# Dense heads of a hybrid encoder: the next head's projections one step fewer, its meta scores one step sooner

## The chip, the cores and the metric

The kernel runs on one core of a Trainium2 chip. The metric is device time in microseconds (us) for one execution of the whole program, median of the runs shown. TensorE is called PE in the profile (its weight loads PEld), VectorE DVE, ScalarE ACT, GpSimd POOL, and the queue of SyncE that issues DMAs SP.

## What is computed

The reference is an encoder trunk of two layers over 1024 real tokens and 16 meta tokens. Each layer is one mixer with three groups of heads side by side: A (window attention), B (dense attention over all tokens) and C (a gated recurrence). The change touches group B alone. Cut to that group:

```python
DEPTH = 2; SEQ = 1024; N_META = 16; BLOCK = 128; HEAD_DIM = 64
B_HEADS = 4; B_QK_DIM = HEAD_DIM; B_V_DIM = 2 * HEAD_DIM

def diff_attention(q, k, v, lam, key_ok):
    """q/k (B,Lp,H,2,d), v (B,Lp,H,2d); dense bidirectional, swept over 128-query blocks."""
    ...
    def attend(q_blk):
        s = jnp.einsum('bqhcd,bkhcd->bhcqk', q_blk, k).astype(jnp.float32) * scale
        s = jnp.where(key_ok, s, NEG)
        p = jax.nn.softmax(s, axis=-1)
        a = p[:, :, 0] - lam * p[:, :, 1]
        return jnp.einsum('bhqk,bkhv->bqhv', a.astype(v.dtype), v)

# in mixer_layer, h = x @ w_in:
qb = rotary(qb.reshape(bsz, lp, 2 * B_HEADS, B_QK_DIM), cos, sin)
kb = rotary(kb.reshape(bsz, lp, 2 * B_HEADS, B_QK_DIM), cos, sin)
ob = diff_attention(qb, kb, vb, lam, valid)
ob = rms_norm(ob, subln_w.reshape(B_HEADS, B_V_DIM)) * (1.0 - lam_init)
yb = ob.reshape(bsz, lp, B_WIDTH).astype(dt) * jax.nn.silu(gb)
```

Each head has two score components. Their softmaxes are combined with a factor lam, and the result weighs the values.

## The kernel before

The kernel has one hand-written instruction stream for each engine, joined by semaphores. The order in a stream is the order of the code; no scheduler moves anything. Matrix products are made in three matmuls each (hi times hi, hi times lo, lo times hi).

Group B is done head by head, in four passes B0 to B3 (`pass_b`). A pass has one step for each block of 128 query tokens: nine in layer 0 (steps 0 to 8, the last one holds the 16 meta tokens as queries) and eight in layer 1 (steps 0 to 7). In the code n is this number and t the step. In step t of head g the engines do the following.

- PE: the scores of the step after (`scores`, twelve matmuls, L1103), then, once DVE has combined the probabilities of step t, nine transposes of them (`transposes`, L1259, in groups 0, 1 and 2) and nine products with the values (`values`, L1275). Between the groups of transposes it makes parts of the projection of the next head nx (`project`, L931).
- ACT: copies of the transposed probabilities (`evac_probs`, L1611), the exponentials of the step after (`exps`, L1599 and L1601, first component 0, then 1), the copy of the output (`values_out`, L1621) and its norm.
- DVE: the maximum of each score component (`maximum`, L2123 and L2124), work for the next head, the output of the step before (`finish`, L2149 and L2152), and the combination of the two components of the step after (`combine`, L2133 to L2139; the long one is L2137).

The next head's queries and keys are projected in units (f, j): piece j of three pieces of tokens (0, 1, 2), f = 0 and 1 for the two halves of each rotated pair. A unit is made in two half-projections of twelve matmuls each. `b_steps` hands them out: it makes the list of halves, divides it over n - 3 steps, and notes for each step which units DVE rotates (`turned`, one step after the unit is complete: `qk_rope`, L2062 to L2068) and which pieces are then split into hi and lo (`rounded`: `qk_hi_of` on ACT, L1574, and `qk_lo` on DVE, L2076). Between rotation and split lie four DMAs of SP for each piece (`place_qk`, from `rot` to `qk_t`). Units (0, 0) and (1, 0) of a head are made at the end of the pass before last, in steps n - 2 and n - 1 (`early`, `after_next`); pass B2 has none to make there, and pass B3 has no next head. The number of half-projections in steps 0, 1, 2, ... is 2, 2, 1, 1, 1, 1, 0, 2, 2 in layer 0 and 2, 2, 2, 1, 1, 0, 2, 2 in layer 1, with 0 in the last two steps of B2.

The scores of the 16 meta keys are made for a whole head at once. In step n - 2, once its keys are complete, DVE copies the meta keys (`meta_keys`, L2087), PE multiplies them with all queries (`meta_scores`, L1213, into banks 6 and 0), and ACT copies the rows to `meta_rows` (L1580). In step n - 1, PE turns the rows (`meta_turned`, L1224, in layer 0 also L1228), ACT copies them to `meta_s` (`meta_out`, L1588 and L1589), and DVE makes their bound (`meta_bound`, L2097 to L2102), which `maximum` needs for the next head's first scores. These stand ahead of the step's other work on each of the three engines. The PSUM banks are given out in the same order by `bank_plan`.

The place of the turning in PE's stream is

```python
scores(b_step(l, g, t, 1))
if nx and t == q_tiles(l) - 1:
    meta_turned(l, nx)
pe.wait_ge(b_comb, B_STEP[l, g, t])
transposes(t, 0)
```

## Time and profile before

| | us |
|---|---|
| median of 3 runs | 1710.3 |
| lowest and highest run | 1707.62, 1711.12 |
| the profiled execution | 1706.29 |
| its span | 1705.0 |
| PE busy in it | 1567.1 |
| DVE, ACT, POOL busy | 1080.7, 875.4, 410.1 |

All times in the rows are from the start of the profiled span. The dense passes of layer 0 lie between about 500 and 798 us, those of layer 1 between about 1338 and 1604. A row of a timeline gives the start, the length from the first to the last of the instructions merged in it, the engine, the line, the operation, what it writes and reads, and their number. A bracket at its end is the time that the engine was idle before it, and what ended that. A row of a window gives the busy time of each engine in it. A timeline can count twice as many values (L1275) as the program's order, since the profile holds two records for each.

### The profile page before, as it was taken

To read this page: it belongs to the slowest core of one execution; us is meant where nothing else is said; L and a number is where in the kernel's file an instruction comes from. 1 tells how busy PE (TensorE), PEld (TensorE's weight loads), DVE (VectorE), ACT (ScalarE), POOL (GpSimd) and SP (SyncE) were. 2 spreads that over 40 slices of the span, in tenths; PEclk is the share of its full clock that TensorE was granted. 3 is DMA by queue.
4 is the path that set the end of the run, shared out by engine and by line. 5 is a ranking of instruction groups with operands and counts; after the bars stand their busy time and mean duration, and the time that the engine had idled before them with its cause. 6 is when DMAs were issued, how large, how long until landed. Compare 5 with 4: busy or idle time off the path is not lost.

```text
span 1705.0 us, 38582 instructions
## 1 busy us (share of the span) xinstructions
PE 1567.1 (92%) x15296; PEld 1463.2 (86%) x15296; DVE 1080.7 (63%) x2461; ACT 875.4 (51%) x2569; POOL 410.1 (24%) x390
## 2 busy tenths in 40 slices
PE   2899999999999989889989999999999899987996
PEld 2899999999888878668989999999999789876896
DVE  6477585446557777775255766844455678787527
ACT  4444545355617676775035445452464477677404
POOL 5333141220121002020453423213103101112044
PEclk9899999999999999999999999999999999999998
DMA  7111201200120111042122102012002111114312
GB/s 264 39 53 37 63 27 32 83 26 14 36 86 17 49 25 49 18 157 99 60 75 83 56 14 64 27 36 78 29 11 71 52 25 50 50 27 146 117 51 100
DMA packets 97859, 102.32 MB, mean 60 GB/s; under 512 B 7504, under 2 KB 87744, under 8 KB 97424
## 3 DMA queue, kind: packets, MB, share of 16 engines
q1 hardware_dynamic: 96720, 98.78, 18.0%
q8 instruction: 123, 2.02, 0.5%
q10 hardware_dynamic: 960, 1.07, 0.2%
q14 instruction: 56, 0.46, 0.1%
HBM read 70.14 MB, written 21.17 MB: 54 GB/s over the span
## 4 chain that ended last, share of the span: by engine, by line
PE 58%; DVE 19%; ACT 11%; POOL 5%; issue 4%; DMA 3%; SPq 0%; ACTq 0%; DVEq 0%; POOLq 0%
PE psum L931 42%; ACT p_b L1601 3%; PE psum L1275 3%; DVE p_b L2137 3%; PE psum L1103 3%; PE psum L1259 3%; POOL w_lo L896 2%; DVE row_max L2123 2%; DVE s_a L1990 2%; PE psum L1000 2%; ACT aT_b L1611 1%; ACT pT_a L1517 1%; POOL w_hi L892 1%; PE psum L978 1%; DMA w_raw<-in_w_in 1%
## 5 line engine op out<-in xcount | busy, mean ns | idle before, releaser
L931 PE MATMUL psum<-w_hi,hT_hi 128*128 128x256 f32 x1824 | 523.6, 287 | 9.4 <-POOL w_lo L896 8.1
L931 PE MATMUL psum<-w_hi,hT_lo 128*128 128x256 f32 x1824 | 513.7, 282 | 0.0
L931 PE MATMUL psum<-w_lo,hT_hi 128*128 128x256 f32 x1824 | 513.5, 282 | 0.0
L892 POOL CAST w_hi<-w_raw 128x512 fp32r<-128x512 f32 (+1 forms) x168 | 112.3, 668 | 1147.8 <-DMA w_raw<-in_w_in 679.6
L931 PEld LDWEIGHTS psum<-w_hi,hT_hi 128*128 128x128 f32 x1824 | 344.2, 189 | 18.5 <-POOL w_lo L896 10.0
L931 PEld LDWEIGHTS psum<-w_hi,hT_lo 128*128 128x128 f32 x1824 | 344.3, 189 | 0.0
L931 PEld LDWEIGHTS psum<-w_lo,hT_hi 128*128 128x128 f32 x1824 | 344.2, 189 | 0.0
L931 PE MATMUL psum<-hT_hi,w_hi 128*128 128x346 f32 (+1 forms) x672 | 226.4, 337 | 9.5 <-DVE hT_lo L1728 9.4
L896 POOL TENSOR_TENSOR w_lo<-w_raw,w_hi 128x512 fp32r<-128x512 f32 (+1 forms) x168 | 215.7, 1284 | 24.1 <-DVE neg_max L2124 12.0
L931 PE MATMUL psum<-hT_hi,w_lo 128*128 128x346 f32 (+1 forms) x672 | 218.1, 325 | 0.0
L931 PE MATMUL psum<-hT_lo,w_hi 128*128 128x346 f32 (+1 forms) x672 | 217.8, 324 | 0.0
L2123 DVE TENSOR_REDUCE row_max<-psum 128x1 f32<-128x1024 f32 x136 | 165.6, 1218 | 16.7 <-PE psum L1103 16.4
L1275 PE MATMUL psum<-vg_b,aT_b 128*128 128x128 f32 (+1 forms) x1224 | 157.1, 279 | 10.0 <-ACT aT_b L1611 10.0
L1275 PEld LDWEIGHTS psum<-vg_b,aT_b 128*128 128x128 f32 (+1 forms) x1224 | 142.8, 186 | 17.4 <-ACT aT_b L1611 14.0
L1601 ACT ACTIVATE p_b<-psum,neg_max 128x1024 f32<-128x1024 f32 x136 | 150.1, 1103 | 0.0
L931 PEld LDWEIGHTS psum<-hT_hi,w_hi 128*128 128x128 f32 x672 | 128.5, 191 | 11.9 <-issue 10.9
L1611 ACT COPY aT_b<-psum 128x384 f32<-128x384 f32 (+1 forms) x204 | 87.6, 463 | 90.9 <-PE psum L1259 89.7
L931 PEld LDWEIGHTS psum<-hT_hi,w_lo 128*128 128x128 f32 x672 | 128.8, 192 | 0.0
L931 PEld LDWEIGHTS psum<-hT_lo,w_hi 128*128 128x128 f32 x672 | 128.3, 191 | 0.0
L1103 PE MATMUL psum<-qk_b 64*128 64x512 f32 (+1 forms) x816 | 113.1, 408 | 13.7 <-ACT p_b L1601 13.3
L1259 PEld LDWEIGHTS psum<-ident,p_b 128*128 128x128 f32 (+1 forms) x612 | 66.3, 140 | 58.1 <-DVE p_b L2137 35.4
L1259 PE MATMUL psum<-ident,p_b 128*128 128x128 f32 (+1 forms) x612 | 92.4, 277 | 25.1 <-DVE p_b L2137 16.9
(179 smaller groups left out, 2382.5 us busy)
## 6 DMA issues: line engine op xcount, KB each, us to landing
w_raw<-in_w_in SPq DMA_DIRECT2D x72, 256.0 KB, 3.8
w_raw<-in_w_in SPq DMA_DIRECT2D x28, 512.0 KB, 4.4
h_dram<-hbuf SPq DMA_DIRECT2D x16, 512.0 KB, 2.6
w_raw<-in_w_out SPq DMA_DIRECT2D x16, 512.0 KB, 4.3
hbuf<-h_dram SPq DMA_DIRECT2D x16, 512.0 KB, 6.2
qk_b<-y_dram SPq DMA_DIRECT2D x16, 512.0 KB, 3.3
y_dram<-y_stage SPq DMA_DIRECT2D x96, 64.0 KB, 1.6
qk_t<-rot SPq DMA_DIRECT2D x56, 86.5 KB, 2.2
```

Source lines behind the costliest of these rows:

```text
L892: pool.tensor_copy(hi, raw).then_inc(w_hi_done, 1)
L896: pool.tensor_tensor(lo, raw, hi.bitcast(F32), ALU.subtract).then_inc(w_split, 1)
L931: last = nc.tensor.matmul(out_ap, lhs[a](k), rhs[b](k), start=k == 0 and a + b == 0, stop=k == KT - 1 and b == 1)
L1000: return nc.tensor.matmul(o_ap, k_sel[rs, k_at:k_at + H_ROWS], q_ap, start=True, stop=True)
L1103: last = [nc.tensor.matmul(out_of(r), q_of(a, r), k_of(b, r), start=i == 0, stop=i == 2) for r in range(2)]
L1259: last = nc.tensor.transpose(psum[:, b, i * P:i * P + m], p0_b[0:m, B_STEP[l, g, t] % 2, k * P:(k + 1) * P], ident[0:m, 0:m])
L1275: last = nc.tensor.matmul(psum[0:m, b, 0:P], aT_b[:, k, 0:m], vg_b[:, head_no(g), k, 0:P], start=k == 0, stop=k == TILES - 1)
L1601: nc.scalar.activation(probs[:, 0:REAL * P].rearrange("p (i n) -> p i n", i=2), psum[0:m, b:b + 2, :], ACT.Exp, scale=SCALE, bias=neg_max[ ...
L1611: nc.scalar.copy(aT_b[:, 3 * j:3 * j + 3, 0:m], psum[:, b, 0:3 * P].rearrange("p (k c) -> p k c", k=3)[:, :, 0:m])\
L1990: then(nc.vector.tensor_tensor_reduce(s_a[0:m, i, h, 0:w], psum[0:m, bank(key), 0:w], band_sb[0:m, band_columns(t)], 1.0, NEG, ALU.add, AL ...
L2123: then(nc.vector.tensor_reduce(row_max[0:m, i, c:c + 1], psum[0:m, b:b + 2, :], AX.XY, ALU.max))
L2137: stt(p0_b[0:m, i, 0:TOK], p1_b[0:m, :], coef[0:m, j, 0:1], p0_b[0:m, i, 0:TOK], ALU.mult, ALU.add).then_inc(b_comb, 1)
```

## The change

The halves are divided over n - 4 steps instead of n - 3, and the last piece is split one step sooner (`b_steps`). Half-projections per step become 2, 2, 2, 1, 1, 0, 0, 2, 2 in layer 0 and 2, 2, 2, 2, 0, 0, 2, 2 in layer 1. The meta keys, their scores and the copy of the rows move from step n - 2 to n - 3. Turning, copy and bound move from n - 1 to n - 2: on PE behind the first two groups of transposes, on ACT behind the third copy of probabilities, on DVE behind the maxima. The scores go into banks 6 and 7. For heads B1 to B3 ACT writes the rows into `rot`, the buffer of the rotation. In step n - 2 the second half-projection no longer stands behind the values.

```diff
@@ b_steps
-        q, r = divmod(len(halves), n - 3)
+        q, r = divmod(len(halves), n - 4)
...
-            rounded[min(t + 2, n - 2)] += [j for _, (f, j) in turned[t] if f]
+            rounded[min(t + 2, n - 3)] += [j for _, (f, j) in turned[t] if f]
@@ bank_plan
-                if nx and t == n - 1:
-                    add(("meta", l, nx), 6)
                 add(("aT", l, g, t, 0), 0)
                 add(("aT", l, g, t, 1), 1)
+                if nx and t == n - 2:
+                    add(("meta", l, nx), 6)
...
-                if nx and t == n - 2:
-                    for i, b in enumerate((6, 0)):
-                        add(("metaT", l, nx, i), b)
+                if nx and t == n - 3:
+                    for i in range(2):
+                        add(("metaT", l, nx, i), 6 + i)
@@ meta_rows_of
+        if g != "B0":
+            return rot[0:2 * META].rearrange("p a n -> p (a n)")[:, 0:REAL * P]
@@ tensor, pass_b
-                if nx and t == q_tiles(l) - 1:
-                    meta_turned(l, nx)
                 pe.wait_ge(b_comb, B_STEP[l, g, t])
                 transposes(t, 0)
                 transposes(t, 1)
+                if nx and t == q_tiles(l) - 2:
+                    meta_turned(l, nx)
                 for h, x, half in parts[:1]:
                     project(l, h, "qk", x, half)
                 transposes(t, 2)
-                late = nx and t == q_tiles(l) - 2
                 for h, x, half in parts[1:2]:
-                    if not late:
-                        project(l, h, "qk", x, half)
+                    project(l, h, "qk", x, half)
...
-                if late:
-                    for h, x, half in parts[1:2]:
-                        project(l, h, "qk", x, half)
+                if nx and t == q_tiles(l) - 3:
                     meta_scores(l, nx)
@@ scalar, pass_b
-                if nx and t == q_tiles(l) - 1:
-                    meta_out(l, nx)
...
+                if nx and t == q_tiles(l) - 2:
+                    meta_out(l, nx)
                 if after:
                     exps(after, 1)
...
-                if nx and t == q_tiles(l) - 2:
+                if nx and t == q_tiles(l) - 3:
                     meta_rows_out(l, nx)
@@ vector, pass_b
-                if after and after[1] == 0:
-                    meta_bound(l, after[0])
...
+                if nx and t == q_tiles(l) - 3:
+                    meta_keys(l, nx)
                 if nx and t == q_tiles(l) - 2:
-                    meta_keys(l, nx)
+                    meta_bound(l, nx)
```

PE in the end of pass B2 of layer 0, before. The first row is the end of step 6; `psum<-qk_b` are scores, `ident,p_b` transposes, `vg_b,aT_b` values, and a row x9 of transposes holds all three groups.

```order
L1275 MATMUL psum<-vg_b,aT_b 128x128 x9
L1103 MATMUL psum<-qk_b 16x512 x12
L1259 MATMUL psum<-ident,p_b 128x128 x9
L1275 MATMUL psum<-vg_b,aT_b 128x128 x9
L1213 MATMUL psum<-qk_b,meta_k 32x512 x6
L1103 MATMUL psum<-qk_b 128x512 x12
L1224 MATMUL psum<-ident,meta_rows 128x32 x8
L1228 MATMUL psum<-meta_k,qk_b 16x32 x3
L1259 MATMUL psum<-ident,p_b 128x16 x9
L1275 MATMUL psum<-vg_b,aT_b 16x128 x9
```

The same place in the changed kernel, from the values of step 6 on.

```order
L1277 MATMUL psum<-vg_b,aT_b 128x128 x9
L1215 MATMUL psum<-qk_b,meta_k 32x512 x6
L1105 MATMUL psum<-qk_b 16x512 x12
L1261 MATMUL psum<-ident,p_b 128x128 x6
L1226 MATMUL psum<-ident,rot 128x32 x8
L1230 MATMUL psum<-meta_k,qk_b 16x32 x3
L1261 MATMUL psum<-ident,p_b 128x128 x3
L1277 MATMUL psum<-vg_b,aT_b 128x128 x9
L1105 MATMUL psum<-qk_b 128x512 x12
L1261 MATMUL psum<-ident,p_b 128x16 x9
```

The meta scores stand ahead of the scores of step 8 now instead of ahead of the next head's, and the turning stands behind two groups of step 7's transposes instead of ahead of step 8's.

DVE in step 4 of pass B1 of layer 1, before: the maxima of step 5, the lo half of piece 1, the finish of step 3 and the start of the combination.

```order
L2123 TENSOR_REDUCE row_max<-psum 128x1
L2124 SCALAR_TENSOR_TENSOR neg_max<-row_max,meta_max 128x1
L2123 TENSOR_REDUCE row_max<-psum 128x1
L2124 SCALAR_TENSOR_TENSOR neg_max<-row_max,meta_max 128x1
L2076 TENSOR_TENSOR qk_b<-qk_t,qk_b 128x2x346
L2149 SCALAR_TENSOR_TENSOR coef<-rstd,inv_sum 128x1
L2152 SCALAR_TENSOR_TENSOR y_stage<-o_b,coef,vg_b 128x128
```

The same step in the changed kernel.

```order
L2121 TENSOR_REDUCE row_max<-psum 128x1
L2122 SCALAR_TENSOR_TENSOR neg_max<-row_max,meta_max 128x1
L2121 TENSOR_REDUCE row_max<-psum 128x1
L2122 SCALAR_TENSOR_TENSOR neg_max<-row_max,meta_max 128x1
L2074 TENSOR_TENSOR qk_b<-qk_t,qk_b 128x2x346
L2063 TENSOR_TENSOR rot<-psum,rope_sb 128x346
L2064 TENSOR_TENSOR psum<-psum,rope_sb 128x346
L2065 TENSOR_TENSOR rot<-rot 128x346
L2066 TENSOR_TENSOR rot<-rot,psum 128x346
L2147 SCALAR_TENSOR_TENSOR coef<-rstd,inv_sum 128x1
L2150 SCALAR_TENSOR_TENSOR y_stage<-o_b,coef,vg_b 128x128
```

The four operations of the second rotation of piece 2 came from step 5 to step 4, behind the lo half of piece 1.

## Rows read from the trace of the kernel before

**Rows 1.** Page, part 1: busy us (share of the span) and instructions of each engine.

```profile
PE 1567.1 (92%) x15296; PEld 1463.2 (86%) x15296; DVE 1080.7 (63%) x2461; ACT 875.4 (51%) x2569; POOL 410.1 (24%) x390
```

**Rows 2.** Timeline of PE, pass B1 of layer 1: start us, length us, then the instruction.

```profile
1429.54 0.88 PE L1259 MATMUL psum<-ident,p_b 128*128 128x128 f32 x6
...
1436.48 1.65 PE L1103 MATMUL psum<-qk_b 64*128 64x512 f32 x12
1438.06 0.87 PE L1259 MATMUL psum<-ident,p_b 128*128 128x128 f32 x6
...
1443.21 1.65 PE L1103 MATMUL psum<-qk_b 64*128 64x512 f32 x12
...
1477.21 1.65 PE L1103 MATMUL psum<-qk_b 64*128 64x512 f32 x12
```

**Rows 3.** Timeline of DVE, the same pass: start us, length us, then the instruction.

```profile
1429.65 1.23 DVE L2123 TENSOR_REDUCE row_max<-psum 128x1 f32<-128x1024 f32 x1 [1.49 <-PE psum L1103]
...
1436.40 1.30 DVE L2137 SCALAR_TENSOR_TENSOR p_b<-p_b,coef 128x1040 f32<-128x1040 f32 x1
...
1438.16 1.22 DVE L2123 TENSOR_REDUCE row_max<-psum 128x1 f32<-128x1024 f32 x1 [0.39 <-PE psum L1103]
...
1443.83 1.30 DVE L2137 SCALAR_TENSOR_TENSOR p_b<-p_b,coef 128x1040 f32<-128x1040 f32 x1
...
1451.20 1.30 DVE L2137 SCALAR_TENSOR_TENSOR p_b<-p_b,coef 128x1040 f32<-128x1040 f32 x1
```

**Rows 4.** Timeline of DVE, combinations in B1 of layer 0, then in B0 of layer 1.

```profile
605.38 1.30 DVE L2137 SCALAR_TENSOR_TENSOR p_b<-p_b,coef 128x1040 f32<-128x1040 f32 x1
...
612.50 1.30 DVE L2137 SCALAR_TENSOR_TENSOR p_b<-p_b,coef 128x1040 f32<-128x1040 f32 x1
...
627.01 1.30 DVE L2137 SCALAR_TENSOR_TENSOR p_b<-p_b,coef 128x1040 f32<-128x1040 f32 x1
...
1369.27 1.30 DVE L2137 SCALAR_TENSOR_TENSOR p_b<-p_b,coef 128x1040 f32<-128x1040 f32 x1
...
1377.51 1.30 DVE L2137 SCALAR_TENSOR_TENSOR p_b<-p_b,coef 128x1040 f32<-128x1040 f32 x1
```

**Rows 5.** Timeline of DVE, end of B2 and first steps of B3, layer 0.

```profile
701.00 1.30 DVE L2137 SCALAR_TENSOR_TENSOR p_b<-p_b,coef 128x1040 f32<-128x1040 f32 x1
...
708.12 1.30 DVE L2137 SCALAR_TENSOR_TENSOR p_b<-p_b,coef 128x1040 f32<-128x1040 f32 x1
...
716.24 1.29 DVE L2137 SCALAR_TENSOR_TENSOR p_b<-p_b,coef 16x1040 f32<-16x1040 f32 x1
...
721.19 1.23 DVE L2123 TENSOR_REDUCE row_max<-psum 128x1 f32<-128x1024 f32 x1
...
726.37 1.30 DVE L2137 SCALAR_TENSOR_TENSOR p_b<-p_b,coef 128x1040 f32<-128x1040 f32 x1
...
733.97 1.30 DVE L2137 SCALAR_TENSOR_TENSOR p_b<-p_b,coef 128x1040 f32<-128x1040 f32 x1
...
740.80 1.30 DVE L2137 SCALAR_TENSOR_TENSOR p_b<-p_b,coef 128x1040 f32<-128x1040 f32 x1
```

**Rows 6.** Timeline of PE, layer 0: the first scores in B2, then its end.

```profile
653.38 1.65 PE L1103 MATMUL psum<-qk_b 64*128 64x512 f32 x12
...
716.69 1.67 PE L1103 MATMUL psum<-qk_b 64*128 64x512 f32 x12
718.29 0.68 PE L1224 MATMUL psum<-ident,meta_rows 32*128 32x32 f32 x8
...
724.27 1.05 PE L1275 MATMUL psum<-vg_b,aT_b 128*16 128x128 f32 x6 [2.74 <-ACT aT_b L1611]
725.76 2.74 PE L1103 MATMUL psum<-qk_b 64*128 64x512 f32 x12 [0.43 <-ACT p_b L1601]
```

**Rows 7.** Windows: length, busy PE, PEld, DVE, ACT, POOL, granted clock, DMA share, GB/s.

```profile
1468.05:1477.21 9.16, 9.16 (x72) 8.49 (x71) 5.62 (x17) 5.07 (x13) 0.00 (x0) 1.00 0.03 8
724.70:728.20 3.50, 3.07 (x16) 2.10 (x14) 1.92 (x5) 2.04 (x7) 0.00 (x0) 0.51 0.69 205
```

## The prediction, made before the changed kernel was run

> **What bounds the kernel now.** I read the page first. TensorE is busy for 1567.1 of 1705.0 us [rows 1], so an edit is worth what it adds to or takes from TensorE's idle time in the stretch that it touches. All its matmuls stay. I then read the dense passes step by step, on the timelines of PE and DVE. "comb(t)" is the start of the L2137 row of step t, "S(t)" the start of the twelve L1103 matmuls that make step t's scores, which TensorE issues in step t-1.
>
> Two limits alternate. With two half-projections a step is bound by TensorE: one such step lies between the L1259 rows at 1429.54 and 1438.06, 8.52 us [rows 2], with no idle time noted in it. With one or none it is bound by the ring DVE combine, transposes, ACT copies and exponentials, combine: 7.12 to 7.43 us from comb to comb in the steps with one half-projection [rows 3, 4], 6.83 in pass B3 with none [rows 5], while TensorE has about 6.6 and 4.7 us of work (8.52 less one or two half-projections of some 1.9, below). So a half-projection is free in a step bound by the ring, and costs where it makes TensorE the bound.
>
> The last step of a pass holds the chain that the change goes for: scores, turned rows, ACT's copy of them, DVE's bound, then the maximum. DVE's first maximum for the next head starts at 721.19 [rows 5], where the scores issued at 716.69 [rows 6] would have let it start at 718.37 (1.68 after S, as from 1436.48 in [rows 2] to 1438.16 in [rows 3]): 2.8 us late. But in five of six passes the question is whether TensorE waits for it. In pass B1 of layer 1 it does not: busy 9.16 of 9.16 us in that step [rows 7]. In B2, whose last two steps have no projections, it does: 2.74 us idle before the matmuls at 724.27, and then the granted clock falls to the lower level, 1.2 of 2.4 GHz (0.51 in [rows 7]); the scores at 725.76 take 2.74 us for 1.65 [rows 6].
>
> So the rows show a gap to win in one pass of each layer, and none in the others. The Trainium skill, page Perfetto Trace Analysis, section Optimization Strategy, says to find the gaps of the bound engine and to make what they wait for start sooner. That is what the change does; by that rule the late maximum is won back wherever it stands, which is rival (a), and by [rows 7] there is nothing to win where TensorE has no gap.
>
> **Layer 0, the front of a pass.** Half-projections per step go from 2,2,1,1,1,1,0,2,2 to 2,2,2,1,1,0,0,2,2. Up to step 5 that is exactly what layer 1 does before the change, so layer 1 is the template. comb(3) to comb(4) is 612.50 - 605.38 = 7.12 us in layer 0's B1, a step on the ring, and so it is in B0. In layer 1 it is 1377.51 - 1369.27 = 8.24 in B0, +1.1, and 1443.83 - 1436.40 = 7.43 in B1, +0.3 [rows 3, 4]. In B2 DVE is the later one in both layers: 0. The step that loses its half-projection stays on the ring: 0.
>
> **Layer 0, the end of B0 and B1.** The lo half of the keys, the copies to meta_k and the meta scores now lie in step 6, without projections. For this step B2's step 7 is the template, since it has none either: comb(7) to comb(8) 716.24 - 708.12 = 8.12 us, and S, behind the meta scores, follows 0.45 later, at 716.69 [rows 5, 6]. From comb(6) at 627.01 [rows 4]: + 8.12 + 0.45, then a full step of TensorE 8.52 plus the turned rows (0.68 in [rows 6], about 0.8 with its three extra matmuls), then 8.52 again, is 653.4 for S(1) of the next head. Before it is 653.38 [rows 6]. So +0.0 to +0.3 each; I take +0.1. What the last step gains, step 6 pays: it has nothing left to hide the wait for meta_k.
>
> **Layer 0, the end of B2.** Here the chain is exposed. Before: from comb(6) at 701.00 to comb(1) of B3 at 733.97, 32.97 us [rows 5]. After: 8.12 for step 6; step 7: S at +0.45, maximum 1.68 later, then from first maximum to combine 726.37 - 721.19 = 5.18 us, and, as an estimate from the 0.68 us of turned rows and the 0.45 above, 0.5 each for ACT's copy and DVE's bound between maximum and combine: 8.3; then two plain ring steps of 740.80 - 733.97 = 6.83. Sum 30.1 us: -2.9. Of this about 0.8 is the slow clock: comb to comb is 733.97 - 726.37 = 7.60 there and 6.83 after.
>
> **Layer 1, B0 and B1.** The counts go from 2,2,2,1,1,0,2,2 to 2,2,2,2,0,0,2,2, and no template exists. Step 3 gets its second half-projection and becomes bound by TensorE: S(5) moves from 1443.21 to 1438.06 + (1436.48 - 1429.54) = 1445.00 [rows 2], which is also the price of a half-projection, 1.79 us here, and 0.1 to 0.2 more where it fills no small wait. Step 4 now holds the lo half of piece 1 and the second rope of piece 2 together on DVE, which step 2 also has: from its first maximum at 1429.65 to the combine at 1436.40 is 6.75 us [rows 3]. So comb(5) = 1445.00 + 1.68 + 6.75 = 1453.43. Before it is at 1451.20: 2.2 later. Step 5 takes the 8.12 us of the keys' step, comb(6) = 1461.55. Then S(7) at 1462.00, + 8.52 + 0.68 + 8.52 = 1479.7 for S(1) of the next head, against 1477.21 [rows 2]: +2.5. Two passes: +5.0. The edit moves a half-projection from a step with room into one without, and puts two DVE jobs into one step: TensorE then stands idle in steps 4 and 5 with nothing issued to cover it.
>
> The bounds: if step 4's work on DVE found room and TensorE's slack took the rest, each pass would cost 0. If every growth added up, it would be 1.79 in step 3, 6.75 + 1.30 (the L2137 row) - 7.37 = 0.68 in step 4 and 8.12 - 7.12 = 1.0 in step 5: 3.5. I take the 2.5 of the path traced, since each of its pieces is a row.
>
> **Layer 1, B2.** The same 2.2 at comb(5), less the end's gain of layer 0 without the clock, 2.1: +0.1.
>
> Edits at nothing: meta rows in rot (nothing else is in it then: the last piece's DMAs have landed before ACT's hi copy, and the next rope waits for a projection behind the turned rows); the changed banks 6, 7 (both were released by the rope a step earlier); SP's copies of piece 2 a step sooner (the hi copy waits for the landing, which has as long as it had; if late, it adds to the 8.12).
>
> **Sum.** 1.1 + 0.3 + 0.2 - 2.9 + 5.0 + 0.1 = +3.8 us. The profiled execution took 1706.29 us, 1.3 of it around the span, and would take 1710.1; the median of the three runs is 1710.3, 4.0 above that execution, and the difference is carried over to it: 1714.1.
>
> **Rivals.** (a) Faster: the end chain does count in all six passes, and the 2.8 us of the late maximum come back six times, 16.8 us: 1693.5. For it: the chain is there in every pass. Against: [rows 7], TensorE full. It decides once TensorE waits in that step for more than what step 5 or 6 newly loses, about 2 us. (b) Layer 1 loses nothing, since step 4's two DVE jobs find room: 1.1 + 0.3 + 0.2 - 2.9 + 0 - 2.1 = -3.4: 1706.9. For it: DVE is idle in part of every step. Against: 6.75 us in step 2 is a chain without a wait. (c) The clock. In layer 0 the scores after a 2.74 us idle gap ran at the lower level of the granted clock [rows 6, 7]. Layer 1's two steps without projections could bring such a drop into each pass: 3 x 1.1 and the 0.8 that B2 no longer saves: 1714.1 + 4.1 = 1718.2. Against: the gaps that I work out for these steps are under 2 us. The Trainium skill, page TensorE: Matmul & The Clock Gate, section HAM oscillation — how this bites in real kernels, says that waits in which TensorE idles bring its clock down and that each costs again. By that rule (c) is a real danger, and the drop of layer 0 agrees with it.
>
> **The numbers.** The forecast, +3.8 with +1.5 to +6.5, 0.65; (a) 0.07; (b) 0.14; (c) 0.14. Runs of this kernel can be told apart from about 0.2%, 3.4 us. Faster is (a) and a third of (b): 0.11. Within 0.2% is two fifths of the forecast and the rest of (b): 0.36. Slower is the rest: 0.53. The range reaches from (b) to (c): 1707 to 1718.5; (a) is left out, and so are the outer halves of (b) and (c).
>
> **What would show it.** In layer 1, B0 and B1: comb(4) to comb(5) near 9.6 us instead of 7.4, comb(5) to comb(6) near 8.1 instead of 7.1, and the last two steps shorter, with the pass 2 to 3 us longer. In layer 0's B2: the combine before the next head 7 us after its predecessor instead of 10.1, no clock record at half there. In B0 and B1 the last step shorter by two, and step 6 longer by 1. I am wrong if the layer 1 passes don't grow, or if TensorE was waiting in the last steps after all.

## The result and the profile after

| | before | after |
|---|---|---|
| median of 20 runs each, on one chip | 1709.95 | 1714.43 |
| ratio after to before, 95% interval | | 1.003, 1.0022 to 1.0039 |
| the profiled execution, its span | 1706.29, 1705.0 | 1715.02, 1713.7 |
| mean granted clock of that execution | 0.990 | 0.988 |

The change costs 4.5 us by the medians. These are over all runs; the ratios, here and below, leave out the few slow runs (one of before here, at 2025 us). First the place that the forecast put the most on, pass B1 of layer 1. These are DVE's combinations (L2135 in the changed kernel, L2137 before) of steps 3 to 7, then the maximum and combinations that open the next head:

```profile
1442.76 1.30 DVE L2135 SCALAR_TENSOR_TENSOR p_b<-p_b,coef 128x1040 f32<-128x1040 f32 x1
...
1450.18 1.30 DVE L2135 SCALAR_TENSOR_TENSOR p_b<-p_b,coef 128x1040 f32<-128x1040 f32 x1
...
1459.67 1.30 DVE L2135 SCALAR_TENSOR_TENSOR p_b<-p_b,coef 128x1040 f32<-128x1040 f32 x1
...
1467.85 1.30 DVE L2135 SCALAR_TENSOR_TENSOR p_b<-p_b,coef 128x1040 f32<-128x1040 f32 x1
...
1476.78 1.30 DVE L2135 SCALAR_TENSOR_TENSOR p_b<-p_b,coef 128x1040 f32<-128x1040 f32 x1
1479.33 1.23 DVE L2121 TENSOR_REDUCE row_max<-psum 128x1 f32<-128x1024 f32 x1 [1.18 <-PE psum L1105]
...
1485.00 1.30 DVE L2135 SCALAR_TENSOR_TENSOR p_b<-p_b,coef 128x1040 f32<-128x1040 f32 x1
```

From comb(4) to comb(5) it is now 9.49 us where it was 7.37 [rows 3], and to comb(6) 8.18. On PE the same stretch reads (timeline; L1105 are scores, L1261 transposes, L1277 values, L1215 the meta scores):

```profile
1451.36 1.65 PE L1105 MATMUL psum<-qk_b 64*128 64x512 f32 x12
...
1456.86 0.94 PE L1277 MATMUL psum<-vg_b,aT_b 128*128 128x128 f32 x6 [0.82 <-ACT aT_b L1609]
1458.34 1.65 PE L1105 MATMUL psum<-qk_b 64*128 64x512 f32 x12 [0.55 <-ACT p_b L1599]
1461.02 0.88 PE L1261 MATMUL psum<-ident,p_b 128*128 128x128 f32 x6 [1.04 <-DVE p_b L2135]
...
1466.77 1.57 PE L1215 MATMUL psum<-qk_b,meta_k 128*32 128x512 f32 x6 [1.52 <-DVE meta_k L2085]
```

S(5) is at 1451.36, 1.18 behind comb(4). Before it was at 1443.21, 0.62 ahead of it [rows 2, 3]. And TensorE, with no projections in these two steps, waits 0.82, 0.55, 1.04 and 1.52 us in the rows shown. The gain at the end is there too: the last step, from 1476.78 to 1485.00, takes 8.22 us for 10.37, and the next head's first maximum, at 1479.33, starts 1.69 behind its scores (1477.64), without the lateness of before. The step ahead of it, from 1467.85, is not shorter but longer, 8.93 for 8.59.

Next the end of B2 in layer 0, DVE from comb(6) to comb(1) of the next head, the answer to [rows 5]:

```profile
703.95 1.30 DVE L2135 SCALAR_TENSOR_TENSOR p_b<-p_b,coef 128x1040 f32<-128x1040 f32 x1
...
712.14 1.30 DVE L2135 SCALAR_TENSOR_TENSOR p_b<-p_b,coef 128x1040 f32<-128x1040 f32 x1
...
721.92 1.29 DVE L2135 SCALAR_TENSOR_TENSOR p_b<-p_b,coef 16x1040 f32<-16x1040 f32 x1
723.21 1.20 DVE L2121 TENSOR_REDUCE row_max<-psum 128x1 f32<-128x1024 f32 x1
...
728.37 1.30 DVE L2135 SCALAR_TENSOR_TENSOR p_b<-p_b,coef 128x1040 f32<-128x1040 f32 x1
...
735.19 1.30 DVE L2135 SCALAR_TENSOR_TENSOR p_b<-p_b,coef 128x1040 f32<-128x1040 f32 x1
```

The maximum of the next head follows at once on the combination (723.21), and that step takes 6.45 us instead of 10.13. But the step from 712.14 to 721.92 takes 9.78. PE's timeline shows why. The first window is the stretch ahead of the meta scores, the other two give the clock at the same place of B0 and here (columns as in [rows 7]; the sixth figure after the length is the granted clock):

```profile
711.05 2.60 PE L1215 MATMUL psum<-qk_b,meta_k 128*32 128x512 f32 x6 [1.52 <-DVE meta_k L2085]
713.58 2.05 PE L1105 MATMUL psum<-qk_b 64*16 64x512 f32 x12
```

```profile
705.25:711.05 5.80, 3.79 (x27) 3.10 (x27) 4.24 (x12) 5.13 (x15) 0.00 (x0) 1.00 0.16 40
...
561.10:564.50 3.40, 3.40 (x10) 1.10 (x12) 2.29 (x7) 1.85 (x6) 0.00 (x0) 0.50 0.07 19
711.30:714.70 3.40, 3.40 (x12) 1.08 (x12) 2.11 (x6) 1.67 (x4) 0.00 (x0) 0.50 0.07 19
```

Behind the 1.52 us wait for the meta keys the granted clock is at 0.50, the lower level of 1.2 GHz. The six meta scores take 2.60 us for the 1.57 that they take at 1466.77, and the scores behind them 2.05 (1.57 at full clock, at 638.10 in B1). The drop that [rows 7] showed at 724.7 is gone, and two others have come, this one and one at 561 in B0. Of the six waits of this kind in the changed kernel (one in each pass, all 1.52 us long) two are followed by a drop, though TensorE is busy for 3.79 or 3.80 of the 5.80 us ahead of each of the six. In B2 the kernel before has the same wait one step later, and no drop behind it, so the rows from which the forecast built this stretch ran at full clock. On PE's timeline of before:

```profile
715.19 1.57 PE L1213 MATMUL psum<-qk_b,meta_k 128*32 128x512 f32 x6 [1.52 <-DVE meta_k L2087]
```

The passes one by one. A pass is taken from comb(1) of its head to comb(1) of the next, B0 from comb(0), so that the ends of the passes count where they are felt; for B1 of layer 1 after the change that is 1493.86 - 1424.91 = 68.95:

```profile
1424.91 1.30 DVE L2135 SCALAR_TENSOR_TENSOR p_b<-p_b,coef 128x1040 f32<-128x1040 f32 x1
...
1493.86 1.30 DVE L2135 SCALAR_TENSOR_TENSOR p_b<-p_b,coef 128x1040 f32<-128x1040 f32 x1
```

The forecast's terms stand beside the difference.

| us | before | after | difference | forecast |
|---|---|---|---|---|
| layer 0, B0 | 79.14 | 81.78 | +2.6 | +1.2 |
| layer 0, B1 | 73.61 | 74.04 | +0.4 | +0.4 |
| layer 0, B2 | 72.93 | 71.47 | -1.5 | -2.9 |
| layer 1, B0 | 73.18 | 75.26 | +2.1 | +2.5 |
| layer 1, B1 | 65.82 | 68.95 | +3.1 | +2.5 |
| layer 1, B2 | 64.54 | 64.59 | +0.05 | +0.1 |
| sum | 429.2 | 436.1 | +6.9 | +3.8 |

The rest of the program, whose code the change leaves alone, differs by 1.8 us between these two executions (8.7 of span less 6.9). Such a difference says nothing of the change: the changed kernel profiled a second time (changed_again below) has the same dense passes to 0.1 us and a span of 1708.1, 5.6 us less than here.

### The profile page after: what moved, and what is told of

It is laid out like the page before. It is cut to its first block, busy times and chain, and to the rows that moved or that the text cites. A ratio compares the mean times of both kernels' runs of the same rounds, so it can differ in the third digit from the quotient of the medians.

```text
span 1713.7 us, 38582 instructions
## 1 busy us (share of the span) xinstructions
PE 1573.2 (92%) x15296; PEld 1463.7 (85%) x15296; DVE 1081.2 (63%) x2461; ACT 875.4 (51%) x2569; POOL 409.8 (24%) x390
## 3 DMA queue, kind: packets, MB, share of 16 engines
q10 hardware_dynamic: 960, 1.07, 0.2%
## 4 chain that ended last, share of the span: by engine, by line
PE 60%; DVE 18%; ACT 10%; POOL 5%; issue 3%; DMA 3%; SPq 0%; ACTq 0%; DVEq 0%; POOLq 0%
PE psum L933 43%; PE psum L1277 4%; PE psum L1105 4%; PE psum L1261 3%; ACT p_b L1599 3%; POOL w_lo L898 2%; DVE p_b L2135 2%; ACT aT_b L1609 2%; DVE s_a L1988 2%; DVE row_max L2121 2%; PE psum L1002 2%; POOL w_hi L894 1%; ACT pT_a L1515 1%; PE psum L980 1%; DMA w_raw<-in_w_in 1%
## 5 line engine op out<-in xcount | busy, mean ns | idle before, releaser
L1277 PE MATMUL psum<-vg_b,aT_b 128*128 128x128 f32 (+1 forms) x1224 | 158.8, 279 | 8.9 <-ACT aT_b L1609 8.9
L1277 PEld LDWEIGHTS psum<-vg_b,aT_b 128*128 128x128 f32 (+1 forms) x1224 | 143.6, 186 | 17.8 <-ACT aT_b L1609 14.1
L1105 PE MATMUL psum<-qk_b 64*128 64x512 f32 (+1 forms) x816 | 112.9, 408 | 13.9 <-ACT p_b L1599 13.8
L1261 PEld LDWEIGHTS psum<-ident,p_b 128*128 128x128 f32 (+1 forms) x612 | 65.8, 140 | 57.4 <-DVE p_b L2135 26.8
L1261 PE MATMUL psum<-ident,p_b 128*128 128x128 f32 (+1 forms) x612 | 92.7, 278 | 22.2 <-DVE p_b L2135 13.1
```

The source lines that it names most:

```text
L1105: last = [nc.tensor.matmul(out_of(r), q_of(a, r), k_of(b, r), start=i == 0, stop=i == 2) for r in range(2)]
L1261: last = nc.tensor.transpose(psum[:, b, i * P:i * P + m], p0_b[0:m, B_STEP[l, g, t] % 2, k * P:(k + 1) * P], ident[0:m, 0:m])
L1277: last = nc.tensor.matmul(psum[0:m, b, 0:P], aT_b[:, k, 0:m], vg_b[:, head_no(g), k, 0:P], start=k == 0, stop=k == TILES - 1)
```

## The experiments

All ratios are to the kernel before, run beside it on the same chip, with 95% intervals. "Layer 0" and "layer 1" are sums of three passes as in the table above (before: 225.7 and 203.5; after: 227.3 and 208.8). The texts written ahead of the runs name kernels by labels: e4_filler is experiment 4, e6_split_bound is 7, e7_b2_only is 8, e9_b2_filler is 9 and e11_bound_and_filler is 11.

**1. The distribution of the halves alone.** Edit to the kernel before; meta scores, turning and bound stay where they were.

```diff
-        q, r = divmod(len(halves), n - 3)
+        q, r = divmod(len(halves), n - 4)
```

> Only the half-projections are handed out one step sooner; the meta scores, their turning and their bound stay where they were before. Theory (a half-projection is free on the ring and costs in a step bound by TensorE, and layer 1's step 4 gets two DVE jobs): layer 0 +1.4 us as in its front, layer 1 comb(5) 2.2 later in each pass and step 5 then 0.3 shorter, so +1.9 in each of three passes: about +7 us against the kernel before, more than the whole change. Rival (moving halves costs nothing, what costs is the moved meta work): 0, within 0.1%.

Measured: 1716.77 (1.0039, 1.0023 to 1.0055); layer 0 +0.5, layer 1 +6.0. Combinations of steps 4 to 7 and 0 of the next head in B1 of layer 1:

```profile
1450.09 1.30 DVE L2137 SCALAR_TENSOR_TENSOR p_b<-p_b,coef 128x1040 f32<-128x1040 f32 x1
...
1459.57 1.30 DVE L2137 SCALAR_TENSOR_TENSOR p_b<-p_b,coef 128x1040 f32<-128x1040 f32 x1
...
1466.31 1.30 DVE L2137 SCALAR_TENSOR_TENSOR p_b<-p_b,coef 128x1040 f32<-128x1040 f32 x1
...
1474.89 1.30 DVE L2137 SCALAR_TENSOR_TENSOR p_b<-p_b,coef 128x1040 f32<-128x1040 f32 x1
...
1485.25 1.30 DVE L2137 SCALAR_TENSOR_TENSOR p_b<-p_b,coef 128x1040 f32<-128x1040 f32 x1
```

Step 4 costs 9.48 us here as in the full change, step 5, without the meta keys, 6.74, and the last step keeps its 10.36. Pass by pass (B0, B1, B2 of layer 1) the halves alone cost 1.6, 2.1 and 2.3 us, the full change 2.1, 3.1 and 0.05. So most of the loss comes from the halves, but not all of it: the sooner chain adds 0.5 and 1.0 in B0 and B1, where step 5 takes 8.18 us for 6.74 and the next head's first step 8.9 for 8.0, more than the last step gives back (8.22 for 10.36). In B2 the chain takes 2.3 back, and 0.9 of that is clock: in this trace alone the clock fell at 1551 us, and the first step of B3 takes 7.73 us for the 6.84 of before.

```profile
1552.34 1.30 DVE L2137 SCALAR_TENSOR_TENSOR p_b<-p_b,coef 128x1040 f32<-128x1040 f32 x1
...
1560.07 1.30 DVE L2137 SCALAR_TENSOR_TENSOR p_b<-p_b,coef 128x1040 f32<-128x1040 f32 x1
```

Layer 0 lost 0.5 us and not the 1.4 expected. The front came as expected, but step 6, left without a half-projection, takes 6.74 us for 7.12, 0.4 less in each of the three passes. The forecast has this term at 0.

**2 and 3. The change in one layer only.** Each place that the change touches asks for the layer and takes the old form in the other:

```diff
+SOONER = {0}
-        q, r = divmod(len(halves), n - 4)
+        q, r = divmod(len(halves), n - 4 if l in SOONER else n - 3)
...
```

> The whole change in layer 0 alone, layer 1 as before. By the forecast's sum: 1.1 + 0.3 + 0.2 - 2.9 = -1.3 us against before. By the trace of the changed kernel, where two scores or meta scores rows in step 6 of layer 0 ran at the lower clock: +1.6 us, if these drops come in most executions. Rival: the cost of the change is spread over both layers alike: +2.5.

> The whole change in layer 1 alone, layer 0 as before. By the forecast and by the trace of the changed kernel: +5.1 us against before (2.5 in B0, 2.5 in B1, 0.1 in B2). Rival, alike in both layers: +2.5.

Measured: layer 0 only 1709.17 (0.9993, 0.9978 to 1.0007), with layer 0 at -1.4 and layer 1 at -0.1 in its trace; layer 1 only (the same with {1}) 1716.21 (1.0041, 1.0025 to 1.0057), with +5.2 in layer 1. In the first trace the clock fell at none of the three waits of layer 0: the six meta scores take 1.57, 1.57 and 1.59 us there. The same code at the same waits had two drops in the trace of the full change. So -1.4 is what layer 0 gains where no new drop comes, almost to the tenth the forecast's sum for it (1.1 + 0.3 + 0.2 - 2.9 = -1.3). It holds pass by pass too: B0 +1.2, B1 +0.4, B2 -3.0, for +1.2, +0.4 and -2.9. Against this trace the full change is 1.5 longer in B0 and 1.5 in B2, the price of a drop.

**4. Work in place of the wait.** Six matmuls that nobody reads, ahead of TensorE's wait for the meta keys of heads B1 to B3, in the changed kernel:

```diff
         def meta_scores(l, g):
+            if g != "B0":
+                wait_free(pe, ("metaT", l, g, 0))
+                for _ in range(6):
+                    nc.tensor.matmul(psum[0:2 * META, bank(("metaT", l, g, 0)), :], hT_hi[:, 0:2 * META],
+                                     hT_hi[:, 0:512], start=True, stop=True)
             pe.wait_ge(b_keys, 4 * B_HEAD[l, g])
```

> The changed kernel, with six extra matmuls of 32x512 (their result is overwritten) in the wait of step n - 3 for the copies to meta_k, where TensorE stands idle for 1.52 us. They take some 1.3 us, so they should hide in the wait. If the granted clock falls because of the idle time in steps 5 and 6 of layer 0, the drops at 561 and 711 us go and the time falls by 1.5 us for each, 2 to 3 us below the changed kernel. If the drops have another cause, or don't come often, it stays as the changed kernel, +5 us against before.

Measured: 1710.85 (1.0009, 0.9996 to 1.0022). The end of B0 of layer 0 on PE's timeline and the clock there:

```profile
558.56 1.62 PE L1213 MATMUL psum<-hT_hi 128*32 128x512 f32 x6
560.32 1.59 PE L1220 MATMUL psum<-qk_b,meta_k 128*32 128x512 f32 x6
561.84 1.57 PE L1105 MATMUL psum<-qk_b 64*16 64x512 f32 x12
```

```profile
558.50:562.00 3.50, 3.36 (x17) 1.37 (x18) 3.12 (x11) 3.16 (x11) 0.00 (x0) 1.00 0.08 23
```

The filler takes 1.62 us (1.3 were expected) in a place where TensorE waited 1.52, the meta scores start no later (7.10 us behind comb(6) with it and without), and they run at full clock. Layer 0 comes to 224.56, 2.7 us less than in the changed kernel, and layer 1, which had no drop, stays at 208.79. The median is 3.6 below the changed kernel's (the intervals of these two ratios touch at 1.0022). So the work added costs nothing. That it holds the clock is not shown by this one trace, since experiment 2 had no drop in layer 0 either. The means over the runs speak for it: a granted clock of 0.991 here (11 runs) against 0.988 for the changed kernel (32 runs, its repeat below included).

**5 and 6. What makes step 4 of layer 1 longer.** First, DVE's second job taken out of it: piece 1 is split a step sooner.

```diff
@@ b_steps, the changed kernel
+        if l == 1:
+            rounded[3].append(rounded[4].pop(rounded[4].index(1)))
```

> The changed kernel, but in layer 1 the hi and lo split of piece 1 is done in step 3 instead of 4, so that step 4 holds only the second rotation of piece 2 on DVE, and step 3, where DVE waits for late scores anyway, takes the split. If the two DVE jobs in step 4 are part of the loss, comb(4) to comb(5) falls from 9.5 to about 8.7 us (less the 0.8 of the lo half) and layer 1 gains 0.8 in each of three passes: 2.4 us below the changed kernel. If step 4 is long only because its scores come late behind the second half-projection, it stays at 9.5.

Then, the half-projection taken out of step 3 (nine of its twelve matmuls are left out, three are left):

```diff
@@ tensor, project, the changed kernel
+            if l == 1 and half == 1 and x == (1, 2):
+                ks = [KT - 1]
```

> The changed kernel with 9 of the 12 matmuls left out of the second half of layer 1's unit (1, 2), which step 3 makes (the keys of piece 2 are so incomplete). TensorE is freed of 1.45 us in the step which the forecast calls bound by TensorE. If that is what makes comb(5) late, comb(4) to comb(5) falls from 9.5 to 8.05 us, and layer 1 by 1.45 in each pass, 4.3 us below the changed kernel. Rival: the ring and DVE set step 4, and the freed time turns into a wait of TensorE: 0.

Measured, from comb(4) to comb(5) of B1: 7.37 before, 9.49 after, 8.44 with the split sooner, 8.07 with the half-projection gone. The rows of DVE for the last two, the split first:

```profile
1448.63 1.30 DVE L2137 SCALAR_TENSOR_TENSOR p_b<-p_b,coef 128x1040 f32<-128x1040 f32 x1
...
1457.07 1.30 DVE L2137 SCALAR_TENSOR_TENSOR p_b<-p_b,coef 128x1040 f32<-128x1040 f32 x1
```

```profile
1450.18 1.30 DVE L2137 SCALAR_TENSOR_TENSOR p_b<-p_b,coef 128x1040 f32<-128x1040 f32 x1
...
1458.25 1.30 DVE L2137 SCALAR_TENSOR_TENSOR p_b<-p_b,coef 128x1040 f32<-128x1040 f32 x1
```

Both causes are there. Without the half-projection the step falls by 1.42, and 0.70 stay over the old 7.37, where the prediction's bounds put the second job of DVE at 0.68. Without the second job it falls by 1.05, 1.07 stay, and step 3 grows by 0.26. So the half-projection alone makes 1.07, the second job alone 0.70, and both together 2.12, which is 0.35 more than their sum. Whole kernels: 1712.62 (1.002, 1.0007 to 1.0034) with the split sooner, layer 1 at 206.38, 2.4 less than after; and 1710.92 (1.0007, 0.9992 to 1.0022) without the half-projection, where B1 of layer 1 is 1.4 shorter than after, while B0 and B2 of it show no gain: in that execution the clock fell behind the waits for the meta keys of just these two passes (its six meta scores take 2.60 and 2.71 us there), and at no place of layer 0, where this kernel is the same as the changed one.

**7. The bound alone, without moving anything else.** In the kernel before, the part of `meta_bound` for a component stands behind that component's first maximum, which no longer waits for it:

```diff
@@ vector, maximum, the kernel before
+                if t == 0 and g != "B0":
+                    meta_bound(l, g, [c])
@@ vector, pass_b
-                if after and after[1] == 0:
-                    meta_bound(l, after[0])
```

> The kernel before, with one edit of its own: the bound of the next head's meta scores is made for one component at a time, behind the reduction of that component's scores, not for both ahead of it. The exponentials of the next head's first step can start 1.4 to 2 us sooner. TensorE waits for them only at the end of the B2 passes: -1.4 and the 0.8 of the slow clock in layer 0, -1.3 in layer 1, and 0.3 in layer 0's B0, where comb(0) of B1 came late: 3 to 4 us below the kernel before. If the late maximum cost TensorE time in every pass, it would be 1.4 six times, 8 us or more. If it costs nothing anywhere, 0.

Measured: 1708.34 (0.9991, 0.998 to 1.0003); layer 0 -1.4, layer 1 -1.0, the latter in B2 alone. This tests rival (a) by itself. Of the 2.8 us of the late maximum it wins 1.3 to 1.7 in each last step. In B1 of layer 1 the last step does shrink: combinations of steps 7 and 0 of the next head, and the window of the stretch between them:

```profile
1470.40 1.30 DVE L2139 SCALAR_TENSOR_TENSOR p_b<-p_b,coef 128x1040 f32<-128x1040 f32 x1
...
1479.48 1.30 DVE L2139 SCALAR_TENSOR_TENSOR p_b<-p_b,coef 128x1040 f32<-128x1040 f32 x1
```

```profile
1471.70:1480.70 9.00, 9.00 (x73) 8.29 (x73) 6.71 (x18) 5.10 (x13) 0.00 (x0) 1.00 0.11 26
```

It is 9.08 us instead of 10.37, and the pass is 65.90 instead of 65.82: TensorE was busy for all of the stretch, so DVE's earlier combination waits for it in the steps behind. The 1.3 us come back only where TensorE stood idle, in B2 (last step 10.13 to 8.77 in layer 0, 9.65 to 8.19 in layer 1). The passes give 2.3 us and the medians 1.1, less than the 3 to 4 expected. A part is that in layer 0 the clock still fell behind the end of the pass (0.8 of the sum expected).

**8 to 12. The change only where it gains.** The whole change for head B3 of layer 0 (made in pass B2), and the split bound of the kernel above for all others (b2_only):

```diff
+SOONER = {(0, "B3")}
-        q, r = divmod(len(halves), n - 4)
+        q, r = divmod(len(halves), n - 4 if (l, nx) in SOONER else n - 3)
...
```

> The whole change in pass B2 of layer 0 alone, the only pass in which the forecast has it gain (-2.9), and in all other passes the kernel before with the split bound of e6_split_bound. Expected 4.5 us below the kernel before (2.9 + 1.3 + 0.3), 1706 by the median. Rival: front and end of B2 eat what e6_split_bound gives there, no better than that kernel.

Measured: 1705.35 (0.9978, 0.9966 to 0.9991). The median is 4.1 us below the kernel before, for 4.5 expected. Layer 0 comes to 223.70, layer 1 to 203.78. The clock fell behind the wait for the meta keys at 709 us, and also at 1535 in B2 of layer 1, where this kernel has the order of before. Then come four more kernels: the same with the six matmuls of the filler ahead of that wait, for head B3 of both layers (9, b2_filler); the changed kernel again (10, changed_again); the split bound and the filler without any change of order (11, bound_and_filler); and b2_only again (12, b2_again):

> The change kept for the last head of layer 0's third pass alone, the bound split by component in the other heads (both as in e7_b2_only), and six matmuls with no reader (one 32x512 product per component, of sizes as in e4_filler) put on TensorE ahead of its wait for the meta keys in that one head. Theory (the wait for the meta keys lets the granted clock fall at that step, which costs about 1.5 us where it happens, and the filler takes that wait's place): no clock record at half between 700 and 715 us, the six meta scores 1.6 us and not 2.6, the pass over the third head of layer 0 about 1.4 us shorter than in e7_b2_only (71.27 to about 69.9), and the time 0.5 to 1.5 us below e7_b2_only's 1705.35, so a ratio of about 0.997. Rival (the clock falls at times that no step decides, and the filler only adds its own 1.6 us less the wait of 1.5): the time of e7_b2_only within 0.3 us.

> The changed kernel once more, unedited, beside e9_b2_filler on the same chip. Theory (its place in the program and not chance makes the clock fall in the step that makes the meta scores): records at half near 561 and near 711 us again, dense segments of layer 1 again 5.2 us longer than before's, and a ratio of 1.003. Rival (those two drops were this one execution's): neither record there, and layer 0's dense heads 1.4 us shorter than before's, with the ratio still near 1.002.

> The kernel before with the bound split by component (as in e6_split_bound) and the six matmuls with no reader ahead of the wait for the meta keys of the fourth head, in both layers: e9_b2_filler without the changed order of layer 0's third pass. Theory (the changed order is worth 0.7 us in that pass where no clock drop disturbs either, and the late bound leaves TensorE idle a step later, where the clock still falls): a record at half near 725 us, the pass over layer 0's third head about 71.9 us against 69.74 in e9_b2_filler, layer 1 as in e9_b2_filler, and the time some 2 us above the 1700.12 of e9_b2_filler: ratio 0.996. Rival (the filler and the split bound alone did it): within 0.7 us of e9_b2_filler.

> e7_b2_only once more, unedited, on the same chip as e11_bound_and_filler: e9_b2_filler came out 5.2 us below it in another call, of which the dense segments of the two traces show 3.0 (1.5 in the third pass of each layer, where e7's clock fell). Theory (a part of the 5.2 is chance between executions): 1704 to 1706 here, and a drop at half near 709 us again, while the one near 1535 us need not come back. Rival (the filler is worth 5 us): 1705 again with both drops.

| | median | ratio, interval | layer 0 | B2 of it | layer 1 |
|---|---|---|---|---|---|
| b2_only | 1705.35 | 0.9978, 0.9966 to 0.9991 | 223.70 | 71.27 | 203.78 |
| b2_again | 1705.45 | 0.9973, 0.9964 to 0.9983 | 223.67 | 71.21 | 202.40 |
| bound_and_filler | 1705.92 | 0.9983, 0.9974 to 0.9992 | 224.51 | 72.10 | 202.65 |
| b2_filler | 1700.12 | 0.9947, 0.9935 to 0.9959 | 222.14 | 69.74 | 202.30 |
| changed_again | 1714.24 | 1.0025, 1.0013 to 1.0037 | 227.32 | 71.49 | 208.73 |

b2_filler has five runs, the others twelve each. The changed kernel's dense passes repeat to the tenth, with its two drops in the same two passes: 557.05 and 707.03 are the meta scores of B0 and B2 in its trace.

```profile
557.05 2.53 PE L1215 MATMUL psum<-qk_b,meta_k 128*32 128x512 f32 x6 [1.52 <-DVE meta_k L2085]
...
632.55 1.59 PE L1215 MATMUL psum<-qk_b,meta_k 128*32 128x512 f32 x6 [1.52 <-DVE meta_k L2085]
...
707.03 2.36 PE L1215 MATMUL psum<-qk_b,meta_k 128*32 128x512 f32 x6 [1.52 <-DVE meta_k L2085]
```

With change and filler (b2_filler) the end of B2 runs at full clock throughout, from comb(6) to comb(1) of the next head:

```profile
700.98 1.30 DVE L2160 SCALAR_TENSOR_TENSOR p_b<-p_b,coef 128x1040 f32<-128x1040 f32 x1
...
709.17 1.30 DVE L2160 SCALAR_TENSOR_TENSOR p_b<-p_b,coef 128x1040 f32<-128x1040 f32 x1
...
717.43 1.29 DVE L2160 SCALAR_TENSOR_TENSOR p_b<-p_b,coef 16x1040 f32<-16x1040 f32 x1
...
723.88 1.30 DVE L2160 SCALAR_TENSOR_TENSOR p_b<-p_b,coef 128x1040 f32<-128x1040 f32 x1
...
730.77 1.30 DVE L2160 SCALAR_TENSOR_TENSOR p_b<-p_b,coef 128x1040 f32<-128x1040 f32 x1
```

29.79 us, where the prediction's working for this stretch gave 30.1 and the changed kernel needs 31.24. The filler without the change of order (bound_and_filler) does not do it: TensorE then runs dry one step later, and the scores of the next head are slow.

```profile
721.23 0.83 PE L1280 MATMUL psum<-vg_b,aT_b 128*16 128x128 f32 x6 [0.78 <-ACT aT_b L1616]
723.33 2.50 PE L1103 MATMUL psum<-qk_b 64*128 64x512 f32 x12 [1.27 <-ACT p_b L1606]
```

So in this pass the two parts need each other: the order moves the chain away from the pass's end, and with the filler no drop came behind the wait for the meta keys. B2 is 2.4 us shorter with both than with the filler alone (69.74 against 72.10), and 1.5 shorter than with the order alone. This kernel beats the one before by 0.5% and the changed one by 0.8%. The gain is larger than the 0.5 to 1.5 us below b2_only that were expected, and bound_and_filler stayed short of its expected 0.996.

**Open.** The medians of b2_filler and b2_again differ by 5.3 us, their dense passes by 1.6 (and by 3.0 from b2_only's). The rest lies outside the dense passes, where the two programs are the same. There b2_again's clock fell at 944 and at 1295 us, and b2_filler's did not. The kernel with the filler in all heads had no drop at these two places either, but nor had the kernel before, and bound_and_filler, with its filler, had both. Over the runs the mean granted clock was 0.991 for the two kernels that have the filler wherever the order is changed (16 runs), 0.988 for the changed one (32), and 0.989 for b2_only with its repeat (24), for bound_and_filler (12) and for the kernel changed in layer 0 only (11), whose trace has no drop in the dense passes either. Whether a drop avoided in the dense passes also saves later ones, or chance did it, these runs do not settle.

## Why the prediction was right, and where it was not

The forecast was 1714.1, +3.8 us; measured were 1714.43, +4.5. The interval of the ratio is 3.8 to 6.7 us over 1709.95, so the forecast's +3.8 is at its lower edge. What failed is the price of the moved wait in TensorE's clock, which the forecast put at nothing and which was 1.5 us in each of two passes, and the sign for the second last step of layer 1, which grew.

- **Layer 1, B0 and B1: held.** +5.2 for the two passes against +5.0. The signs named came out: comb(4) to comb(5) 9.49 (near 9.6), comb(5) to comb(6) 8.18 (near 8.1), the last step 8.22 for 10.37. One did not: of the last two steps the first got longer, 8.93 for 8.59. The pieces held: S(5) moved by 1.80 relative to comb(4), and 1.79 was the price of a half-projection. The growth of step 4, 2.12, needs both causes, as the path traced has it (experiments 5 and 6), and undoing the moved chain does not remove it (experiment 1). The 8.12 for step 5, the keys' step, measured 8.18; experiment 1 shows that this term is the chain's and costs more than the 1.0 reckoned, 1.45, since without it the step would have fallen to 6.74.
- **Layer 1, B2: held.** +0.05 for +0.1. Both terms of the sum held: comb(5) came 2.1 later relative to comb(4), for 2.2, and from comb(5) to comb(1) of the next head it is 29.66 us instead of 31.80, the 2.1 forecast. The rows of before, then of after:

```profile
1517.68 1.30 DVE L2137 SCALAR_TENSOR_TENSOR p_b<-p_b,coef 128x1040 f32<-128x1040 f32 x1
...
1549.48 1.30 DVE L2137 SCALAR_TENSOR_TENSOR p_b<-p_b,coef 128x1040 f32<-128x1040 f32 x1
```

```profile
1528.78 1.30 DVE L2135 SCALAR_TENSOR_TENSOR p_b<-p_b,coef 128x1040 f32<-128x1040 f32 x1
...
1558.44 1.30 DVE L2135 SCALAR_TENSOR_TENSOR p_b<-p_b,coef 128x1040 f32<-128x1040 f32 x1
```

- **Layer 0, B1: held** (+0.4). The last step is 3.6 shorter (7.28 for 10.85), where the sign said two. The steps ahead of it grow by 2.2 (step 6 by 1.07, for the 1 forecast) and the first step of the next head by 1.9, so the pass comes out as forecast.
- **Layer 0, B2: the mechanism held, the size did not**, -1.5 for -2.9. The combine before the next head came 6.45 us after its predecessor, as the sign asked, and the drop at 724.7 was gone. The term that failed is the 8.3 us for step 7: it was put together from rows at full clock, and took 9.78, since the clock fell behind the wait for the meta keys. Without the drop it is 8.26 (717.43 - 709.17 in b2_filler), and 8.29 in the kernel changed in layer 0 only. The sentence on the cost of the moved wait ("it has nothing left to hide the wait for meta_k") priced the wait in TensorE's time and not in its clock.
- **Layer 0, B0: the same omission**, +2.6 for +1.2. Without the drop it is +1.2 (experiment 2).
- **Rival (a), faster: fell.** By [rows 7] there was nothing to win where TensorE has no gap. The split bound shows it on its own: last step 1.3 shorter, pass no shorter. The prediction derives this rival from the Trainium skill, page Perfetto Trace Analysis, section Optimization Strategy. That section starts from the gaps of the bound engine, so it does not say that a late maximum is won back where there is no gap, and the traces agree with it as it stands: only the two B2 passes, which had a gap, gained by 1 us or more.
- **Rival (b), layer 1 loses nothing: fell**, +5.2.
- **Rival (c), the clock: half right.** The mechanism was there, at the moved wait, and at 1.5 us a drop instead of 1.1. But it came in two passes of layer 0 and not in three of layer 1 (with the half-projection gone, in two of layer 1), and the argument against it, that gaps under 2 us would not do it, was wrong: the wait in front of both drops is 1.52 us. The Trainium skill, page TensorE: Matmul & The Clock Gate, section HAM oscillation — how this bites in real kernels, speaks of waits for DMAs longer than that; the traces here show that a wait of 1.52 us for VectorE, behind shorter ones (0.97, 0.24 and 0.19 in B2), is enough, sometimes.

The sum came out near the median for a reason that is luck in part. The dense passes cost 6.9 us in the profiled executions, two drops of 1.5 more than the 3.8 forecast, and the medians differ by 2.4 less than that (the ratio 1.003 would be 5.1 us, 1.8 less). No run shows that the drops come in every execution, nor where the 2.4 went. The profiled execution of before had a clock (0.990) above the mean of its repeated runs (0.988), so a difference of two single executions is too large here.

## What to carry to other kernels

Count idle time of the bound engine before moving a chain: a late dependency is worth its lateness only where that engine stands still. The bound's sooner place alone gave 1.0 and 1.2 us in two of six passes and 0.2 or less in the other four. A transfer of work between steps is paid by the step that receives it: here one half-projection and one DVE job together cost 2.1 us a step, and the step relieved gave back 0.4. Where a move leaves TensorE a step with several waits, price the clock as well, and if the wait can't go, try matmuls that nobody reads in its place.

## What the runs showed of the hardware

- The granted clock fell to 0.50 behind a wait of 1.52 us. TensorE was busy for 3.79 of the 5.80 us ahead of the meta scores (window 705.25:711.05). The 1.52 us are most of the rest. Each such drop cost 1.5 us in the pass.
- Which of several equal waits draws a drop is not in the wait itself, nor in TensorE's work just ahead of it. The changed kernel, its repeat and the kernel with the sooner split each had two drops behind six such waits, in B0 and B2 of layer 0. The kernel changed in layer 0 only had none behind the same three waits, with the same 3.80 of 5.80 us busy ahead of the one in B2 (its window is below), and another had its two in layer 1. Over all traces 11 of 42 waits of 1.52 us for the meta keys were followed by a drop.

```profile
702.91:708.71 5.80, 3.80 (x27) 3.11 (x27) 4.24 (x12) 5.12 (x15) 0.00 (x0) 1.00 0.13 33
```

- With six 32x512 matmuls (1.62 us) in the place of that wait no drop came behind it in any of the ten places where they stood, seven of them in the sooner order. In bound_and_filler, with the old order, the clock fell one step later instead. Since 31 of the 42 waits drew no drop even without the filler, ten traced places alone don't prove it; the mean granted clock over the runs (0.991 for 0.988) and the medians of experiments 4 and 9 stand beside them.
